# Up-projections with the high weights against both token parts in one 512-column matmul

## The reference, cut to what matters

```python
def sqrelu_mlp(x, w1, w2):
    return jnp.square(jax.nn.relu(x @ w1)) @ w2
```

## Time and profile before

| | |
|---|---|
| three runs, us | 1413.78, 1412.26, 1413.38 (median 1413.38) |
| profiled execution, first to last instruction | 1409.8 us (its own total is not given; the median of the runs is 3.6 us above) |
| TensorE matmul busy | 1355.4 us (96%) |
| DVE, ACT busy | 871.6 us (62%), 661.7 us (47%) |
| POOL busy | 110.3 us (8%) |
| up matmuls in `slab_up`, three lines | 1544 each |
| down matmuls in `down_part`, three lines | 432 each |

### The profile page before, as it was taken

One profiled execution on the slowest core, in us unless ns is written; L12 is line 12 of the kernel. 1 busy time (PEld: TensorE's weight loads), 2 busy tenths in 40 slices (PEclk: granted clock), 3 DMA queues, 4 the chain that ended last, 5 costly groups with the idle time before them and its releaser, 6 DMA issues.

```text
span 1409.8 us, 20784 instructions
## 1 busy us (share of the span) xinstructions
PE 1355.4 (96%) x8456; PEld 1195.9 (85%) x8456; DVE 871.6 (62%) x936; ACT 661.7 (47%) x777; POOL 110.3 (8%) x146
## 2 busy tenths in 40 slices
PE   8978999999999999999997999999999999999997
PEld 5866899997987899999884788899999998899996
DVE  3767755556577755555577554776666544676664
ACT  3454444444743444444553352655555442555552
POOL 2031100000131100000113000100000100000000
PEclk9999999999999999999998999999999999999999
DMA  7650655555452565553741052565556452366551
GB/s 236 202 210 30 210 196 191 179 184 174 155 170 95 197 206 188 197 181 120 230 173 60 31 194 90 174 206 188 188 197 211 165 163 77 120 211 208 179 179 60
DMA packets 149326, 233.42 MB, mean 166 GB/s; under 512 B 3992, under 2 KB 103568, under 8 KB 149264
## 3 DMA queue, kind: packets, MB, share of 16 engines
q1 hardware_dynamic: 144640, 217.07, 46.6%
q0 software_dynamic: 4336, 14.77, 3.1%
q10 hardware_dynamic: 288, 0.72, 0.1%
HBM read 231.49 MB, written 1.05 MB: 165 GB/s over the span
## 4 chain that ended last, share of the span: by engine, by line
PE 81%; DVE 8%; DMA 4%; ACT 4%; issue 2%; POOL 1%; POOLq 0%; SPq 0%; DVEq 0%; ACTq 0%
PE ps L1598 13%; PE ps L1603 13%; PE ps L1599 13%; PE ps L1617 7%; PE ps L1618 7%; PE ps L1619 7%; PE ps L1550 3%; DMA raw<-in_hy_w_in 3%; PE ps L1552 3%; PE ps L1551 3%; DVE wl L956 2%; PE ps L1577 2%; PE ps L1579 2%; PE ps L1578 2%; PE ps L1777 2%; ACT wh L596 2%
## 5 line engine op out<-in xcount | busy, mean ns | idle before, releaser
L956 DVE TENSOR_TENSOR wl<-raw,wh 128x2048 fp32r<-128x2048 f32 x201 | 461.0, 2296 | 290.9 <-ACT wh L596 290.7
L596 ACT ACTIVATE wh<-raw 128x2048 fp32r<-128x2048 f32 x205 | 392.1, 1915 | 270.6 <-PE ps L1603 90.0
L1598 PE MATMUL ps<-xh,wh 128*128 128x256 f32 x1544 | 380.0, 284 | 3.0 <-DVE xl L969 2.3
L1599 PE MATMUL ps<-xh,wl 128*128 128x256 f32 x1544 | 378.7, 283 | 0.0
L1598 PEld LDWEIGHTS ps<-xh,wh 128*128 128x128 f32 x1544 | 295.9, 192 | 6.5 <-issue 4.3
L1599 PEld LDWEIGHTS ps<-xh,wl 128*128 128x128 f32 x1544 | 296.1, 192 | 2.1 <-issue 0.2
L1603 PE MATMUL ps<-xl,wh 128*128 128x256 f32 x1544 | 216.7, 283 | 0.0
L1603 PEld LDWEIGHTS ps<-xl,wh 128*128 128x128 f32 x1544 | 199.2, 192 | 0.0
L1617 PE MATMUL ps<-wh,hh 128*128 128x512 f32 x432 | 168.8, 391 | 0.4 <-DVE hl L1153 0.4
L1618 PE MATMUL ps<-wl,hh 128*128 128x512 f32 x432 | 168.7, 390 | 0.0
L1619 PE MATMUL ps<-wh,hl 128*128 128x512 f32 x432 | 168.1, 389 | 0.0
(11 more groups left out here) (212 smaller groups left out, 1499.3 us busy)
## 6 DMA issues: line engine op xcount, KB each, us to landing
raw<-in_ffn_w SPq DMA_DIRECT2D x64, 1024.0 KB, 5.2
raw<-in_ffn_w_up SPq DMA_DIRECT2D x44, 1024.0 KB, 5.1
raw<-in_ffn_w_down SPq DMA_DIRECT2D x22, 1024.0 KB, 5.0
raw<-in_xattn_w_kv SPq DMA_DIRECT2D x16, 1024.0 KB, 5.3
raw<-in_gla_w_in SPq DMA_DIRECT2D x13, 1024.0 KB, 5.3
raw<-in_hy_w_in SPq DMA_DIRECT2D x12, 1024.0 KB, 5.2
raw<-in_xattn_w_q SPq DMA_DIRECT2D x8, 1024.0 KB, 5.5
raw<-in_xattn_w_o SPq DMA_DIRECT2D x8, 1024.0 KB, 5.2
```

What stands on the lines that cost most here:

```text
L596: nc.scalar.activation(wh[:, s % RING, :], raw[:, s % RAWS, :], ACT.Copy).then_inc(wh_ready, 1)
L956: nc.vector.tensor_tensor(wl[:, s % RING, :], raw[:, s % RAWS, :], wh[:, s % RING, :].bitcast(F32), ALU.subtract)\
L1598: nc.tensor.matmul(o, wa[:, kt, cs], xh[:, kt, :], start=(kt == 0), stop=False)
L1599: nc.tensor.matmul(o, wb[:, kt, cs], xh[:, kt, :], start=False, stop=False)
```

## The change

In the FFN stages `slab_up` is replaced by `slab_wide`. `xh` and `xl` become the halves of one tile `xhl`, side by side for each kt. Each tile a of a slab gets a PSUM bank of its own. First `wl` x `xh` goes to columns 0 to 255 of both banks (16 matmuls of 256 columns); then each block of `wh` takes `xh` and `xl` in one matmul of 512 columns (16 of these), the first half onto what is there, the second half to columns 256 to 511. The two halves of a bank must be added on reading: ACT copies the second halves of both banks to SBUF, DVE adds the first halves onto them. So a slab needs two banks. In the plain FFN the pairs 0, 1 and 2, 3 alternate; in the gated FFN banks 0, 1 always take the gate and 2, 3 the value. Relu moves into DVE's square. `mid` and `taps` read the sum in SBUF (`u`, one buffer each for gate and value, not doubled). The written order within group g of a gated stage, after:

- ACT: split gate(g+1); copy low gate; split value(g+1); mid gate; copy low value; silu; mid value; split down(g); hh
- DVE: split gate(g+1); sum gate; split value(g+1); taps gate; sum value; split down(g); taps value; product; hl

The other stages keep `slab_up` and their matmuls.

```diff
+        xhl = sb("xhl", [P, KT, 2, T], F32R)
+        xh, xl = xhl[:, :, 0, :], xhl[:, :, 1, :]
+        def halves(b):
+            return [pall[:, b:b + 2, k * T:(k + 1) * T] for k in range(2)]
...
 (ACT, plain FFN)
-                    nc.scalar.activation(r[:, g % 2, :], ps[g % 2][:, :], ACT.Relu).then_inc(bank_free, 1)
+                    nc.scalar.activation(r[:, g % 2].rearrange("p (a t) -> p a t", t=T), halves(2 * (g % 2))[1], ACT.Copy).then_inc(up_low, 1)
...
 (ACT, gated FFN)
+                    act.wait_ge(bank_free, at(i, 8, stage.f0 + 4 + e + 1))
                     for a in range(2):
-                        ins = nc.scalar.activation(dst[:, a, :], bank2(bank)[:, a, :], ACT.Identity,
+                        ins = nc.scalar.activation(dst[:, a, :], u[:, part, a, :], ACT.Identity,
...
-                    mid(2 * (g % 2), cg[:, g % 2], 2 * g, i)
+                    if g:
+                        act.wait_ge(conv_tap, at(i, 16, 2 * (cbase + 2 * g - 1)))
+                    nc.scalar.activation(u[:, 0], halves(0)[1], ACT.Copy).then_inc(up_low, 1)
                     split(up + 1 + LOOKAHEAD if g else up + LOOKAHEAD, i, 12)
-                    act.wait_ge(bank_free, at(i, 8, stage.f0 + 4 + 2 * g + 1))
+                    mid(0, cg[:, g % 2], 2 * g, 2 * g, i)
+                    act.wait_ge(slab_used, at(i, 12, up + 2))
+                    if g:
+                        act.wait_ge(conv_tap, at(i, 16, 2 * (cbase + 2 * g)))
+                    nc.scalar.activation(u[:, 1], halves(2)[1], ACT.Copy).then_inc(up_low, 1)
+                    act.wait_ge(conv_tap, at(i, 16, 2 * (cbase + 2 * g + 1)))
                     nc.scalar.activation(sg[:, g % 2, :], cg[:, g % 2].rearrange("p a t -> p (a t)"), ACT.Silu).then_inc(gate_act, 1)
-                    act.wait_ge(slab_used, at(i, 12, up + 2))
-                    mid(2 * (g % 2) + 1, cv[:, g % 2], FT2 + 2 * g, i)
+                    mid(1, cv[:, g % 2], FT2 + 2 * g, 2 * g + 1, i)
...
 (DVE, plain FFN)
+                    dve.wait_ge(up_low, at(i, 2, lbase + g + 1))
+                    nc.vector.tensor_tensor(r2, halves(2 * (g % 2))[0], r2, ALU.add).then_inc(bank_free, 1)
                     dve.wait_ge(bank_free, at(i, 2, stage.f0 + 4 + g + 1))
-                    nc.vector.tensor_tensor(h[:, g % 2, :], r[:, g % 2, :], r[:, g % 2, :], ALU.mult).then_inc(hid_sq, 1)
+                    nc.vector.scalar_tensor_tensor(h[:, g % 2, :], r[:, g % 2, :], 0.0, r[:, g % 2, :], ALU.max, ALU.mult).then_inc(hid_sq, 1)
...
 (DVE, gated FFN)
+                def sums(part, e, i):
+                    dve.wait_ge(up_low, at(i, 8, lbase + e + 1))
+                    nc.vector.tensor_tensor(u[:, part], halves(2 * part)[0], u[:, part], ALU.add).then_inc(bank_free, 1)
...
-                    taps(2 * (g % 2), cg[:, g % 2], 2 * g, 2 * g, i)
+                    sums(0, 2 * g, i)
                     split(up + 1 + LOOKAHEAD if g else up + LOOKAHEAD, i, 12)
-                    taps(2 * (g % 2) + 1, cv[:, g % 2], FT2 + 2 * g, 2 * g + 1, i)
-                    dve.wait_ge(gate_act, at(i, 4, CV_GROUPS * l + g + 1))
-                    dve.wait_ge(bank_free, at(i, 8, stage.f0 + 4 + 2 * g + 2))
-                    nc.vector.tensor_tensor(h[:, g % 2, :], sg[:, g % 2, :], cv[:, g % 2].rearrange("p a t -> p (a t)"), ALU.mult).then_inc(hid_sq, 1)
+                    taps(0, cg[:, g % 2], 2 * g, 2 * g, i)
+                    sums(1, 2 * g + 1, i)
                     if g < CV_GROUPS - 1:
                         split(up + 2 + LOOKAHEAD if g else up + 1 + LOOKAHEAD, i, 12)
+                    taps(1, cv[:, g % 2], FT2 + 2 * g, 2 * g + 1, i)
+                    dve.wait_ge(gate_act, at(i, 4, CV_GROUPS * l + g + 1))
+                    dve.wait_ge(conv_tap, at(i, 16, 2 * (cbase + 2 * g + 2)))
+                    nc.vector.tensor_tensor(h[:, g % 2, :], sg[:, g % 2, :], cv[:, g % 2].rearrange("p a t -> p (a t)"), ALU.mult).then_inc(hid_sq, 1)
...
 (TensorE, inside slab_wide)
+                for a in range(2):
+                    if stage and a:
+                        pe.wait_ge(bank_free, stage.f0 + 3)
+                    for kt in range(KT):
...
+                        nc.tensor.matmul(ps[bank + a][:, 0:T], wb[:, kt, a * P:(a + 1) * P], xh[:, kt, :], start=(kt == 0), stop=False,
+                                         skip_group_check=True)
+                for a in range(2):
+                    for kt in range(KT):
...
+                        ins = nc.tensor.matmul(ps[bank + a], wa[:, kt, a * P:(a + 1) * P], xhl[:, kt, :, :], start=False, stop=(kt == KT - 1),
+                                               skip_group_check=True)
```

More of the change, by code:

```diff
@@ L183, in build @@
         one_row = sb("one_row", [1, P])
-        ps = [ctx.enter_context(nc.psum_tensor(f"ps{i}", [P, CH], F32)) for i in range(8)]
+        pall = ctx.enter_context(nc.psum_tensor("ps", [P, 8, CH], F32))
+        ps = [pall[:, i, :] for i in range(8)]
+        xh, xl = xhl[:, :, 0, :], xhl[:, :, 1, :]
         ident = con[:, C_IDENT:C_IDENT + P]
@@ L284, in build @@
         sq_done = sem("sq_done")
+        up_low = sem("up_low")
         hid_sq = sem("hid_sq")
@@ L711, in conv, with mid @@
                 cg, cv, sg, h = ar(CV_G, 2, 2, T), ar(CV_V, 2, 2, T), ar(CV_S, 2, CH), ar(CV_H, 2, CH)
-                def mid(bank, dst, ft, i):
+                u = ar(CV_U, 2, 2, T)
+                def mid(part, dst, ft, e, i):
+                    act.wait_ge(bank_free, at(i, 8, stage.f0 + 4 + e + 1))
                     for a in range(2):
                         f = at(i, 8, ft + a)
-                        ins = nc.scalar.activation(dst[:, a, :], bank2(bank)[:, a, :], ACT.Identity,
+                        ins = nc.scalar.activation(dst[:, a, :], u[:, part, a, :], ACT.Identity,
                                                    scale=cw[:, l, 1, bass.ds(f, 1)], bias=cw[:, l, 3, bass.ds(f, 1)])
@@ L915, in _ @@
                     rms_stats(mem, mem_loaded, lambda t: 32)
-                conv(f"conv{l}", l, 2 * SQ_GROUPS + CV_GROUPS * l, 0)
+                conv(f"conv{l}", l, 2 * SQ_GROUPS + CV_GROUPS * l, 2 * CV_GROUPS * l)
                 if l == 0:
@@ L1166, in ffn, with conv @@
                 splits(stage, 2 * g, 2 * g + 1)
-            def conv(name, l, base, cbase):
+            def conv(name, l, base, cbase, lbase):
                 stage = st[name]
@@ L1297, in _ @@
             splits(st["hy_out"], 3, 4)
-            ffn("ffn0", 0)
+            ffn("ffn0", 0, 0)
             ln_ffn(0, 0)
@@ L1482, in _ @@
                     dve.wait_ge(cw_done, 1)
-                conv(f"conv{l}", l, 2 * SQ_GROUPS + CV_GROUPS * l, 2 * CV_GROUPS * l)
+                conv(f"conv{l}", l, 2 * SQ_GROUPS + CV_GROUPS * l, 2 * CV_GROUPS * l, 2 * SQ_GROUPS + 2 * CV_GROUPS * l)
                 w = wait_ffn(st[f"conv{l}"].s0 + 3 * CV_GROUPS, 2 + l)
@@ L1604, in slab_up, with slab_wide @@
                 ins.then_inc(slab_used, 1)
+            def slab_wide(s, bank, i=None, step=0, stage=None):
+                slab(s, i, step)
+                wa, wb = slab_b(wh, s % RING), slab_b(wl, s % RING)
+                if stage:
+                    pe.wait_ge(bank_free, stage.f0 + 2)
+                for a in range(2):
+                    if stage and a:
+                        pe.wait_ge(bank_free, stage.f0 + 3)
+                    for kt in range(KT):
+                        if stage and a == 0 and kt % 4 == 0:
+                            pe.wait_ge(xh_done, 4 * stage.prep + 3 + kt // 4)
+                        nc.tensor.matmul(ps[bank + a][:, 0:T], wb[:, kt, a * P:(a + 1) * P], xh[:, kt, :], start=(kt == 0), stop=False,
+                                         skip_group_check=True)
+                for a in range(2):
+                    for kt in range(KT):
+                        if stage and a == 0 and kt % 4 == 0:
+                            pe.wait_ge(bank_free, stage.f0 + 3 + kt // 4)
+                        ins = nc.tensor.matmul(ps[bank + a], wa[:, kt, a * P:(a + 1) * P], xhl[:, kt, :, :], start=False, stop=(kt == KT - 1),
+                                               skip_group_check=True)
+                ins.then_inc(slab_used, 1)
             def open_down():
@@ L1638, in up @@
                         pe.wait_ge(bank_free, at(i, 2, stage.f0 + g + 3))
-                    slab_up(s0 + 2 * g - 1 if g else s0, g % 2, i=i, step=4, stage=None if g else stage)
+                    slab_wide(s0 + 2 * g - 1 if g else s0, 2 * (g % 2), i=i, step=4, stage=None if g else stage)
                 def down(g, i=None):
@@ L1674, in up @@
                     for a in range(2):
-                        pe.wait_ge(bank_free, at(i, 8, stage.f0 + 2 * g + a + 1))
-                        slab_up(s + a, 2 * (g % 2) + a, i=i, step=12, stage=None if g or a else stage)
+                        pe.wait_ge(bank_free, at(i, 8, stage.f0 + 2 * g + a + 3 if g else stage.f0 + 2 + 2 * a))
```

(1 more changed line is left out.)

24 lines of the change are left out of this document (12 added, 12 removed).

## The result

The changed kernel takes **1445.95 us** (median of four runs, 1444.04 to 1447.10) where the kernel before takes 1413.58 (four runs): ratio 1.0229, 95% interval 1.0215 to 1.0243. The forecast was 1442.4, slower, by a ring in the conv stages (a closed circle of waits between ACT and DVE). The profiled execution has a span of 1442.2 us (1409.8 before).

What follows compares the result with a forecast made beforehand. TensorE's stream of matmuls was taken to bound the kernel. Plain stages -5.3, conv stages +15.6 and +14.7, half clock +4 sum to +29.0 us on 1413.4: 1442.4 us, range 1424 to 1455.

Steps and rivals of the forecast that it cites:

- The stream: TensorE in the FFN stages: an up slab falls from 5.76 to 5.56 us, 15.2 us in all if TensorE stays the bound.
- rival (d): FFN up slabs: the fixed part of a matmul isn't saved, the slab stays at 5.76 us; 1449 us; chance 0.04.
- The plain stages: The two plain FFN stages: shorter up slabs save 3.2 us each, a later hl costs 1.1; together -5.3 us.
- The ring: Conv stages: ACT and DVE wait for each other in a closed circle of 17.8 us a group, against TensorE's 16.57.
- (a): Conv stages: the circle of ACT and DVE stays below TensorE's period of 16.57 us; 1401.5 us; chance 0.10.
- (b): Conv stages: the circle of ACT and DVE equals TensorE's period or is just over; 1412 to 1420 us; chance 0.04.
- Rival (c): Conv stages: slab loads take 7.1 us where 6.2 are covered, 18 us more on all 20 rounds; 1460 us; chance 0.04.
- Head, tail and clock: Conv stages: value mid starts 2.4 us after value(0); TensorE's last wait is about 8 us, half clock then costs about 2.
- the loads' reserve: Conv stages: the down slab's load is issued 6.2 us before ACT wants it and takes 5.0 us, so delays nothing.

## Why the prediction was right, step by step

**The stream**: right. It is 5.56 us an up slab and 11.00 a plain period (11.02 predicted): the fixed part of a matmul is saved in full, and rival (d) fell. The rule of the back-to-back gap that spoke against it (the Trainium skill, TensorE: Matmul & The Clock Gate, Back-to-back issue gap) is contradicted by 0.119 and 0.228 us.

**The plain stages**: -5.1 us against -5.3. The wait at the head of `ffn1` is 1.68 us, where 0.41 + 0.73 + 0.40 = 1.54 was predicted. The last group's chain is 3.4 us, as predicted, and TensorE doesn't wait for it.

**The ring**: right as a mechanism, its circle is the one that was written out, and a copy placed on it or beside it shows it. Rivals (a) and (b) fell: every row that was added up came within 0.02 us but two. They are the mis-sized terms, the last two of the sum:

- From the sum of the value to `mid`: 0.86 us, not 0.73. That price had been read from product to `hh`. In the groups outside the loops (the first and the last two) it is 0.72; the instruction is the same, but inside the loops the column of scale and bias is computed from the loop's counter. That the counter is the reason was not tried by itself.
- From `mid` to ACT's next step: 1.00 us, not 0.92. It reads SBUF now; the bound of +0.04 each was named, and the lower end was taken.

Together they lift the circle from 17.8 to 17.95 us in the looped groups; outside, a round takes 17.65 to 17.70, as the taps of the gate are 0.12 us shorter there as well. In the first stage ten rounds took 1083.16 - 904.22 = 178.9 us where 178 was predicted.

**Rival (c), a load joining the ring**: true in two rounds out of twenty, both in `conv1`, where rounds of 18.24 and 18.50 us stand among those of 17.95 and 17.65. Timeline of ACT in the longer one:

```profile
1398.72 1.92 ACT L602 ACTIVATE wh<-raw 128x2048 fp32r<-128x2048 f32 x1 [1.21 <-DMA raw<-in_ffn_w_up]
```

The other round has a wait of 0.18 us for a down slab at its start. Together they cost 1.1 us: with halved loads, and in the run with warm matmuls, neither wait is there, and the ten rounds of `conv1` (silu to silu) took 177.90 us where the changed kernel took 178.98. The prediction priced it only for all rounds or none.

**Head, tail and clock**: right, the clock partly by luck. The first `mid` of the value came 2.45 us after the first value slab (2.4 predicted). The last wait was 7.91 us (about 8), half clock stood behind it for nine matmuls and cost 7.47 - 5.5 = 2.0 us (2); in `conv1` it cost 1.5 (2). The warm matmuls gave this back. That 2 us came out so closely is luck: in the kernels with such a wait, of 5.3 to 10.7 us, 7 to 13 matmuls ran at half clock, and not more of them after the longer waits. The 1.1 us waits of every group cost no clock. `conv0` came to +18.6 us against 15.6 + 2 = 17.6, the longer circle; `conv1` to +18.2 against 16.7, the longer circle and the two loads less 0.5 us for the clock.

The rest of the difference, 1442.2 - 1438.8 = 3.4 us in the span: 1.0 and 1.5 from the conv stages, 0.2 from the plain ones, and 0.7 from what the change doesn't touch.

**What the prediction didn't see** is how near other rings lie. It named the loads' reserve (6.2 us ahead, 5.0 needed) but not what becomes of it in another order; the missed expectation for the split of down behind the product rests on the same gap.

## What to carry to other kernels

Where several engines run written orders and wait for each other, add up every closed circle from one group to the next, start to start, loads included, and compare it with the bound engine's period; busy shares (64% and 47% here) say nothing of it. Before a step is moved, list everything that hangs on it, the load that its end sets off above all: here two of the three circles went through one. A circle that only equals the bound's period or is a trifle longer (16.60 and 16.74 us beside 16.57) isn't good enough either, since nothing then makes up a late start, and the end pays it, with half clock on top. An order that costs nothing beside one stream (16.61 us beside 16.97) has nothing left once the stream gets shorter (16.57).

## What the runs showed of the hardware that was not expected

- A DVE copy of 512 float32 columns within SBUF takes 0.34 us start to start, a sum of as many, one operand of it in PSUM, 0.60. The Trainium skill (VectorE: DVE Perf Modes, Mode 2×_2P — use both read ports for one tensor) states that an operation with a single tensor operand, in SBUF, uses both read ports and so reaches twice the rate even in fp32, which `tensor_tensor` can't; the trace agrees, fixed part aside.
- A 512 KB load landed in 3.5 us (median of 44) beside 5.1 for 1 MB.
- Idle times of 1.1 us on TensorE, one in every 18 us, left the granted clock at 1.00. After idle times of 5.3 to 10.7 us it was 0.50 for the first 7 to 13 matmuls of 512 columns, 13 after the wait of 5.3 us and 8 after the one of 10.7.
- The same ACT step after a wait started 0.86 us after its releaser inside a loop and 0.72 outside; why was not tried.
